# PEER's first 64 up tiles with one 512-column matmul for the high and low tokens, and routing's second operand in PSUM

## The reference, cut to what matters

```python
q  = (xb @ w_q).reshape(tb, 8, 2, 128)
sc = einsum('thpk,hpnk->thpn', q, sub_keys)          # 8 heads x 2 halves x 128 keys
s1, i1 = top_k(sc[:, :, 0], 16);  s2, i2 = top_k(sc[:, :, 1], 16)
cand = (s1[..., :, None] + s2[..., None, :])         # 256 sums for each head
top_s, pos = top_k(cand, 16)
idx = take_along_axis(i1 * 128 + i2, pos)            # the 16 experts of each head
gw  = softmax(top_s)
act = gelu(einsum('td,thkd->thk', xb, u[idx]))
out = einsum('thk,thkd->td', act * gw, v[idx])
```

## Time and profile before

| | |
|---|---|
| median of three runs | 2038.98 us |
| profiled execution: its time, its span | 2038.0 us, 2036.1 us |
| TensorE's granted clock | 0.998 of full speed |
| TensorE, weight loads busy | 98%, 89% |
| VectorE, ScalarE, GpSimd busy | 61%, 49%, 63% |
| mean DMA rate | 166 GB/s |

### The profile page before, as it was taken

The page is one execution under the profiler, slowest core; times in us unless marked ns, Lnnn a source line. Parts: engine busy times, 40 slices in busy tenths (PEclk is TensorE's granted clock), DMA queues, the critical chain, the costliest instruction groups (busy, mean ns, idle before and its releaser), DMA issues.

```text
span 2036.1 us, 41550 instructions
## 1 busy us (share of the span) xinstructions
PE 1990.1 (98%) x14222; PEld 1821.0 (89%) x14222; DVE 1244.7 (61%) x2722; ACT 992.0 (49%) x1557; POOL 1282.7 (63%) x622
## 2 busy tenths in 40 slices
PE   9999999999999999999999999999999999999998
PEld 9798998999999888888897889999999998888886
DVE  4463399449999544444454624993599994444444
ACT  5545444654443545544555444446444444455444
POOL 6346689876766555555463466998766665555553
PEclk9999999999999999999999999999999999999999
DMA  6524554554444555556545245545444445555554
GB/s 213 164 92 135 177 175 162 179 169 145 146 141 143 185 195 194 189 194 195 186 142 164 82 148 185 172 160 184 165 146 143 145 142 190 194 193 192 192 196 134
DMA packets 93242, 338.45 MB, mean 166 GB/s; under 512 B 10352, under 2 KB 10736, under 8 KB 93168
## 3 DMA queue, kind: packets, MB, share of 16 engines
q1 hardware_dynamic: 93168, 337.53, 49.8%
HBM read 336.44 MB, written 1.05 MB: 166 GB/s over the span
## 4 chain that ended last, share of the span: by engine, by line
PE 91%; POOL 3%; issue 2%; DVE 2%; ACT 1%; DMA 1%; POOLq 0%; SPq 0%; DVEq 0%; ACTq 0%
PE PS L915 34%; PE PS L852 11%; PE PS L857 11%; PE PS L853 11%; PE PS L551 5%; PE PS L866 4%; POOL WL L454 3%; PE PS L535 2%; PE PS L540 2%; PE PS L536 2%; PE PS L777 2%; PE PS L659 1%; PE PS L517 1%; PE PS L588 1%; PE PS L620 0%
## 5 line engine op out<-in xcount | busy, mean ns | idle before, releaser
L454 POOL TENSOR_TENSOR WL<-ring,WH 128x1024 fp32r<-128x1024 f32 x360 | 908.9, 2531 | 413.6 <-ACT WH L1149 207.9
L1149 ACT CAST WH<-ring 128x1024 fp32r<-128x1024 f32 x512 | 538.0, 1051 | 706.1 <-PE PS L915 327.0
L484 POOL TENSOR_TENSOR HL<-G,HH 128x256 fp32r<-128x256 f32 x256 | 372.6, 1456 | 324.1 <-ACT HH L1251 324.0
L1766 DVE TENSOR_TENSOR WL<-ring,WH 128x1024 fp32r<-128x1024 f32 x248 | 303.8, 1225 | 370.9 <-ACT WH L1149 370.9
L852 PE MATMUL PS<-HH,WH 128*128 128x256 f32 x2048 | 512.2, 288 | 0.0
L853 PE MATMUL PS<-HL,WH 128*128 128x256 f32 x2048 | 501.3, 283 | 0.0
L853 PEld LDWEIGHTS PS<-HL,WH 128*128 128x128 f32 x2048 | 392.2, 192 | 0.0
L852 PEld LDWEIGHTS PS<-HH,WH 128*128 128x128 f32 x2048 | 391.2, 191 | 0.0
L915 PE MATMUL PS<-WH,HH 128*128 128x512 f32 x1024 | 315.5, 389 | 3.0 <-issue 3.0
L915 PE MATMUL PS<-WH,HL 128*128 128x512 f32 x1024 | 315.3, 389 | 0.0
L1715 DVE SCALAR_TENSOR_TENSOR OH<-IOB,slotT,PS 128x384 bf16<-128x384 bf16 x512 | 308.0, 602 | 0.0
(11 more groups left out here) (244 smaller groups left out, 2195.0 us busy)
## 6 DMA issues: line engine op xcount, KB each, us to landing
ring<-stream SPq DMA_DIRECT2D x636, 512.0 KB, 3.3
X<-x_t SPq DMA_DIRECT2D x4, 256.0 KB, 3.5
out_t<-X SPq DMA_DIRECT2D x2, 512.0 KB, 2.7
CN<-consts SPq DMA_DIRECT2D x1, 843.5 KB, 9.4
WF<-last SPq DMA_DIRECT2D x1, 512.0 KB, 9.8
PR<-params SPq DMA_DIRECT2D x2, 239.0 KB, 5.0
CN<-consts SPq DMA_DIRECT2D x1, 64.0 KB, 4.3
```

Source lines behind the costliest of these rows:

```text
L454: nc.gpsimd.tensor_tensor(WL[:, b, :], ring[:, slot, :], WH[:, b, :].bitcast(F32), ALU.subtract).then_inc(done, 1)
L484: nc.gpsimd.tensor_tensor(GL[:, s, :], G[:, tile, :], GH[:, s, :].bitcast(F32), ALU.subtract).then_inc(L.gl_ready, 1)
L1149: nc.scalar.copy(WH[:, b, :], ring[:, slot, :]).then_inc(L.hi_ready, 1)
L1766: V.tensor_tensor(WL[:, s % 2, :], ring[:, (U0 + s) % SLOTS, :], WH[:, s % 2, :].bitcast(F32), ALU.subtract).then_inc(L.vlo_ready, 1)
```

## The change

It has three parts.

1. TensorE, up tiles 0 to 63: `wide_in` takes the place of `experts_in`. HH and HL become the two halves of one tensor HX, and WH is multiplied by both in one matmul of 512 moving columns, which fills a whole bank (banks 4 to 7, one tile each): the left half gets high by high, the right half high by low. WL by HH (256 columns) is added to the left half as before.
2. VectorE adds the two halves of the bank into G (`fold`, one a tile), and gelu then works in place on G. TensorE waits for the fold of the tile four earlier, ACT's gelu for the folds of its two tiles. The folds are written into the routing by hand: five in each `top16` on 128 elements (20), fourteen in each token tile's part (28), then the rest up to 56 in a row, and the last eight between the steps up to the one-hots.
3. Routing's operand: the constants 0..15, the second scores and the key indices are copied into PSUM bank 3, and the three operations on 2048 elements (L1668, L1681, L1683) read one operand from there. `EXP_ROUND` goes from 10 to 12 and `TURN_ROUND` from 13 to 14.

```diff
-EXP_ROUND, TURN_ROUND = 10, 13
+EXP_ROUND, TURN_ROUND = 12, 14
-        HH = sb("HH", [P, DC, SEQ], F32R)
-        HL = sb("HL", [P, DC, SEQ], F32R)
+        HX = sb("HX", [P, 2, DC, SEQ], F32R)
+        HH, HL = HX[:, 0, :, :], HX[:, 1, :, :]
...
+        iota_ps = PS[:, 3, 0:TOPK]
+        v_ps = PS[:, 3, 16:16 + P].rearrange("p (h k) -> p h k", h=HEADS)
+        i_ps = PS[:, 3, 256:256 + 2 * P].rearrange("p (h e k) -> p e h k", h=HEADS, e=2)
...
+                    def wide_in(s, ready):
+                        wh, wl = parts(s)
+                        pe.wait_ge(L.hi_ready, ready)
+                        for c in range(DC):
+                            mm = nc.tensor.matmul(bank[4 + s], wh[:, c, :], HX[:, :, c, :], start=(c == 0), stop=False,
+                                                  skip_group_check=True)
+                        mm.then_inc(L.hi_used, 1)
+                        pe.wait_ge(L.lo_ready, ready)
+                        for c in range(DC):
+                            mm = nc.tensor.matmul(bank[4 + s][:, 0:SEQ], wl[:, c, :], HH[:, c, :], start=False,
+                                                  stop=(c == DC - 1), skip_group_check=True)
+                        mm.then_inc(L.piece_done, 1)
...
                             for s in range(SLOTS):
-                                if s % 2 == 0:
-                                    pe.wait_ge(L.gelu_done, r * 2 + (s // 2 - 1))
-                                experts_in(s, r * SLOTS + (s + 1))
+                                pe.wait_ge(L.folded, r * SLOTS + (s - 3))
+                                wide_in(s, r * SLOTS + (s + 1))
...
-                    def gelu(dst, b):
-                        nc.scalar.activation(dst, bank[4 + b].rearrange("p (e n) -> p e n", e=2),
-                                             ACT.Gelu).then_inc(L.gelu_done, 1)
+                    def gelu(acts):
+                        nc.scalar.activation(acts, acts, ACT.Gelu).then_inc(L.gelu_done, 1)
...
                                 high_r(r, s)
                                 if s == 1:
-                                    act.wait_ge(L.piece_done, r * SLOTS + U0)
+                                    act.wait_ge(L.folded, r * SLOTS)
                                 if s == 3:
-                                    act.wait_ge(L.piece_done, r * SLOTS + (U0 + 2))
+                                    act.wait_ge(L.folded, r * SLOTS + 2)
...
+                    def fold():
+                        k = folds[0]
+                        dve.wait_ge(L.piece_done, U0 + k + 1)
+                        V.tensor_reduce(G[:, k, :], bank[4 + k % 4].rearrange("p (a n) -> p n a", a=2), AX.X,
+                                        ALU.add).then_inc(L.folded, 1)
+                        folds[0] += 1
...
+                    V.tensor_copy(iota_ps, cn("iota", 0, TOPK))
                     for t in range(TT):
+                        V.tensor_copy(i_ps.rearrange("p e h k -> p h e k"),
+                                      I16[:, t, :, :].rearrange("p (h e) k -> p h e k", e=2))
+                        step(V.tensor_copy(v_ps, v[:, 1]))
                         step(V.tensor_tensor(CAND[t].rearrange("p h (a b) -> p h a b", a=TOPK),
-                                             bc(v[:, 0], 3, TOPK), bc(v[:, 1], 2, TOPK), ALU.add))
+                                             bc(v[:, 0], 3, TOPK), bc(v_ps, 2, TOPK), ALU.add))
+                        fold()
...
-                            step(V.tensor_tensor(EQ, bc(PAB, 3, TOPK), bc(bc(cn("iota", 0, TOPK), 1, TOPK), 1, HEADS),
+                            step(V.tensor_tensor(EQ, bc(PAB, 3, TOPK), bc(bc(iota_ps, 1, TOPK), 1, HEADS),
                                                  ALU.is_equal))
-                            step(V.tensor_tensor(EQ2, EQ, bc(I16[:, t, :, :].rearrange("p (h e) k -> p e h k", e=2)[:, e], 2, TOPK),
+                            fold()
+                            step(V.tensor_tensor(EQ2, EQ, bc(i_ps[:, e], 2, TOPK),
                                                  ALU.mult))
+                            fold()
...
+                    while folds[0] < TURN_ROUND * SLOTS:
+                        fold()
```

More of the change, by code:

```diff
@@ L1196, in _ @@
                         high_k(k)
-                    act.wait_ge(L.piece_done, U0 + 2)
-                    gelu(G[:, 0:2, :], 0)
+                    act.wait_ge(L.folded, 2)
+                    gelu(G[:, 0:2, :])
                     def rounds_gelu(lo, hi):
@@ L1204, in rounds_gelu @@
                                 if s == 1:
-                                    act.wait_ge(L.piece_done, r * SLOTS + U0)
-                                    gelu(G[:, bass.ds(r * SLOTS - 2, 2), :], 1)
+                                    act.wait_ge(L.folded, r * SLOTS)
+                                    gelu(G[:, bass.ds(r * SLOTS - 2, 2), :])
                                 if s == 3:
-                                    act.wait_ge(L.piece_done, r * SLOTS + (U0 + 2))
-                                    gelu(G[:, bass.ds(r * SLOTS, 2), :], 0)
+                                    act.wait_ge(L.folded, r * SLOTS + 2)
+                                    gelu(G[:, bass.ds(r * SLOTS, 2), :])
                     rounds_gelu(1, EXP_ROUND)
-                    act.wait_ge(L.rt_sub, TT)
+                    act.wait_ge(rt_sub, TT * (layer + 1))
                     nc.scalar.activation(VC[:, :, :, :], VC[:, :, :, :], ACT.Exp).then_inc(rt_exp, 1)
@@ L1239, in _ @@
                     high_k(HK + 1)
-                    act.wait_ge(L.piece_done, U0 + HK)
-                    gelu(G[:, HK - 2:HK, :], 1)
+                    act.wait_ge(L.folded, HK)
+                    gelu(G[:, HK - 2:HK, :])
                     for q in range(HK // 2):
@@ L1642, in _, with top16 @@
                     norm(1, "norm_ffn")
-                    def top16(rows, vals, idxs):
+                    folds = [0]
+                    def fold():
[4 more added lines that the diff above has]
+                        folds[0] += 1
+                    def top16(rows, vals, idxs, folds_at):
                         for r, v in zip(rows, vals):
@@ L1648, in top16 @@
                         step(ins)
-                        for r, v, i in zip(rows, vals, idxs):
+                        fold()
+                        for k, (r, v, i) in enumerate(zip(rows, vals, idxs)):
                             V.max_index(i[:, 0:8], v[:, 0:8], r)
                             ins = V.match_replace(r, v[:, 0:8], r, -3e38)
+                            if k in folds_at:
+                                fold()
                         step(ins)
@@ L1655, in top16 @@
                         step(ins)
-                        for r, v, i in zip(rows, vals, idxs):
+                        fold()
+                        for k, (r, v, i) in enumerate(zip(rows, vals, idxs)):
                             ins = V.max_index(i[:, 8:16], v[:, 8:16], r)
+                            if k == 3:
+                                fold()
                         step(ins)
@@ L1664, in _ @@
                             top16([S[:, t, b, :] for b in bs], [V16[:, t, b, :] for b in bs],
-                                  [I16[:, t, b, :] for b in bs])
+                                  [I16[:, t, b, :] for b in bs], (2, 5))
+                    V.tensor_copy(iota_ps, cn("iota", 0, TOPK))
                     for t in range(TT):
                         v = V16[:, t, :, :].rearrange("p (h e) k -> p e h k", e=2)
+                        V.tensor_copy(i_ps.rearrange("p e h k -> p h e k"),
+                                      I16[:, t, :, :].rearrange("p (h e) k -> p h e k", e=2))
+                        step(V.tensor_copy(v_ps, v[:, 1]))
                         step(V.tensor_tensor(CAND[t].rearrange("p h (a b) -> p h a b", a=TOPK),
-                                             bc(v[:, 0], 3, TOPK), bc(v[:, 1], 2, TOPK), ALU.add))
+                                             bc(v[:, 0], 3, TOPK), bc(v_ps, 2, TOPK), ALU.add))
+                        fold()
                         top16([CAND[t][:, h, :] for h in range(HEADS)], [VC[:, t, h, :] for h in range(HEADS)],
-                              [PC[:, t, h, :] for h in range(HEADS)])
+                              [PC[:, t, h, :] for h in range(HEADS)], (1, 4, 7))
+                        fold()
                         step(V.tensor_copy(esum[:, 0:8], VC[:, t, :, 0]))
                         V.tensor_tensor(VC[:, t, :, :], VC[:, t, :, :], bc(esum[:, 0:8], 2, TOPK),
-                                        ALU.subtract).then_inc(L.rt_sub, 1)
+                                        ALU.subtract).then_inc(rt_sub, 1)
                         for e in range(2):
@@ L1693, in _ @@
                                         bc(esum[:, 8:16], 2, TOPK), ALU.mult).then_inc(L.rt_ready, 1)
+                    while folds[0] < TURN_ROUND * SLOTS:
+                        fold()
```

(11 more changed lines are left out.)

15 lines of the change are left out of this document (9 added, 6 removed).

## The result

The changed kernel takes 2053.92 us in the median of four runs (2053.29 to 2054.39), the kernel before 2038.45 on the same chip. The ratio is 1.0078, 95% interval 1.0066 to 1.0090, so 15.5 us slower. The forecast was 2043 with a range of 2026 to 2054; measured as a change it was 4 us, and is 15.5. The direction and most of the steps held, the size did not.

What follows compares the result with a forecast made beforehand. TensorE, busy 98%, was taken as the bound, then VectorE's lateness: the gain of 6.7 + 8.3 us a layer is spent again, 2.4 more a layer, 2 x 2.4 on 2038.0 is 2042.8, forecast 2043, range 2026 to 2054.

Steps and rivals of the forecast that it cites:

- The tile of 2.776 us: TensorE's 64 up tiles: joined matmuls at 0.227 each make a tile 0.104 less than 2.88, 6.7 us a layer.
- The fold at 0.69 and its 0.594 of VectorE's time: VectorE's sum of 512 elements in PSUM takes 0.687 us and occupies the engine 0.594; upper bound 1.13.
- the rival in which the hop costs more: VectorE's fold over 0.80 us makes VectorE slow from the first fold on, 2051 to 2068; chance 0.14.
- The large operations at 2.29: L1681, L1683 and L1668, with one operand in PSUM, take 2.29 each without port waits; 7.3 us a token tile go.
- The bare 41.3 us of a token tile: VectorE's routing 32.4, copies 0.55 and 14 folds at 0.594, without port waits: 2.95 a tile against TensorE's 2.776.
- GpSimd's lockouts of TensorE gone: In the 64 up tiles TensorE gets back the 8.3 us a layer that it lost to GpSimd.
- VectorE the clock of TensorE: In the token tiles' part a fold may be 2.4 us late; beyond that TensorE follows VectorE, 3.33 us a tile.
- exp and its table loads exposed behind fold 45: At round 12 ACT's exp with two table loads, 3.0 us, has no slack to hide in behind the late fold.
- I take 5.3 for the three: Port waits of the subtraction (L1673) and two PABs (L1678, L1680): 5.3 us a token tile, making it 46.6.
- the chain from fold 45: Fold 45 seen at 387.2, then gelu 0.7, exp with table loads 3.0 and cast 1.05: tile 48 starts at 392.1.
- VectorE nearly keeping up: Rival: small operations wait only 0 to 2 us a token tile, routing ends at 382 to 386, 2023 to 2030; chance 0.22.
- the bound 7.2 for three: Upper bound of the port waits of the subtraction and two PABs in a token tile, where 5.3 was taken.

Runs made afterwards that it cites:

- e1: Changed kernel with the copy and both PABs written to PSUM, so four small VectorE operations avoid the port: 2025.84 us, ratio to before 0.9941.
- e5: Kernel before with only the third part, the three large operations' operands in PSUM, narrow tiles, no folds: 2022.19 us, ratio 0.9923.
- e3: Changed kernel with each gelu of the first 64 tiles one pair later in ACT's queue, behind the casts: 2026.10 us, ratio 0.9941.
- e9: Changed kernel with 23, 23 and 13 filler matmuls ahead of tiles 32, 46 and 48, in the length of the idle stretches: 2054.14 us, ratio 1.0075.

## Why the prediction was wrong

*What held.* The tile of 2.776 us (2.793 measured: eight joined matmuls take 1.84, 0.230 each, for the 0.227 of the earlier trace rows). The fold at 0.69 and its 0.594 of VectorE's time (0.61 by the starts), though it hops 1 KB an element; the rival in which the hop costs more falls. The Trainium skill's 1.73 ns a column ("Vector Engine (DVE) Microarchitecture Reference", Measured stream behaviour on trn2) was the wrong figure to take from that section: it stands for an operation with two sources in SBUF. The same section tells of a one-source operation whose read alternates between two regions at every element, as the fold's does, and which ran at the full rate. The trace agrees, 0.688 us for 512 elements in PSUM. The large operations at 2.29. The bare 41.3 us of a token tile (41.4 in e1). GpSimd's lockouts of TensorE gone (16.0 us in e5 against 16.6). VectorE the clock of TensorE from the first token tile on, seen through the gelu that stands ahead of the cast, with exp and its table loads exposed behind fold 45.

*The step that failed* is the term "I take 5.3 for the three (between 0 and 7.2; the rows show 4.3, and GpSimd is more closely packed now)". It was 7.7 us a token tile, in four operations. For the three that the prediction names the size was nearly right: they waited 5.6 us (2.2, 2.2 and 1.3). The error is the fourth, the copy L1715, whose wait of 2.1 us the sum put at nothing. Its row of before stood at 0.17 us in all four records, and I left it out, though it too goes from SBUF to SBUF and waits when GpSimd is at work. The rule I had quoted myself, that a copy can hold the pair, names it (the Trainium skill, "SBUF — State Buffer", Who interferes with whom; the trace agrees, 2.25 us).

The mechanism behind the size was only half in the prediction, which had GpSimd back to back "where it catches up" and random arrivals otherwise. But the change makes a chain: VectorE comes late, ACT's gelu waits for its fold and holds two casts back, ACT then issues them together, GpSimd makes its low parts in a run without gaps (9.54 us for four), and the small operations, each of which is issued when the last is through, wait a whole GpSimd operation each. That makes VectorE later still. e3 and e5 show the same instructions waiting 1.0 to 1.9 us in a token tile where GpSimd's work is spaced, and e1 shows that the runs stay when the waits are gone. That is how a late fold costs more than its lateness.

*In numbers, first layer.* Routing ended at 398.0, forecast 392.9: 2 x 2.4 for the waits and 0.3 at the start. Tile 48 began at 397.2, forecast 392.1, the same 5.1, so the chain from fold 45 was right. From there to tile 64 it took 46.8 for 45.7: 0.3 for tiles of 2.793, and up to 0.7 for the low clock at tile 48, by what e9 gained. Together 6.2 us over the forecast. The second layer, where tile 48 ran at full clock, came out 5.6 over it: 11.8 in both, for the 11.6 between the forecast 2042.8 of a profiled execution and its 2054.4. Of this 9.6 are the waits in the four token tiles, and 8.3 the copy's alone.

*The range.* I put 0.22 on VectorE nearly keeping up and had no case in which all the small operations are caught, though it was written down as the bound 7.2 for three. By my own chain that bound alone would have given some 2050, and with the copy's 2.1 us some 2051 from the 5.3 as it stood. That the measured 2053.92 lies just inside 2026 to 2054 is luck: the range's upper end was drawn for rivals that did not come, the slow fold above all, and the change was 15.5 us where 4 was forecast.

## What to carry to other kernels

Before work is put on an engine with 28 us to spare, add up its work in the stretch where the new duty falls due, not over the span: 41.3 us of VectorE's work for 38.9 of TensorE's was already too much. When an engine that must wait for another's operations, as VectorE for GpSimd's here, becomes late, recompute the waits with the other side's work in bunches, for every instruction of the kind that can wait, also those whose rows show no wait yet. And issue what others wait for (the cast) ahead of what itself waits (the gelu); that alone was worth 28 us here, as much as taking all four small operations off the port, and both together 42.

## What the hardware showed that was not expected

- A VectorE copy of 8 elements a partition, SBUF to SBUF, takes 0.17 us or 2.25 us, by whether GpSimd is in the middle of its low part; written to PSUM it takes 0.16 (e1).
- A 512-column fp32r matmul whose moving operand is in two runs of 256 columns, 8 KB apart, costs 0.230 us in place of 0.227.
- TensorE's granted clock was 0.50 to 0.53 while the eight matmuls behind idle stretches of 5.3, 5.3 and 3.2 us ran (3.45 to 3.78 us for 2.00), and 1.00 in the stretch from 342 to 386 us. Behind 2.3 us of idling, ahead of tile 48 in the second layer, it was 1.00.
- The lower clock at tiles 32 and 46 moved tile 48 by nothing, as filler showed (397.35 us with it, 397.18 without).
